# Products of a differential head issued one per tile, its outputs kept two tiles later

## The reference

```
s1 = q1 @ k1.T * scale;  s2 = q2 @ k2.T * scale          # inner width 64
p  = softmax(s1) - lam * softmax(s2)
d_out = p @ v                                            # [512, 128] a head
d_out = rms_norm(d_out, subln_g) * (1 - lambda_init)
mix = concat([mla_out, d_out]) @ w_out
```

## Time and profile before

| | us |
|---|---|
| median of three runs | 1977.25 |
| lowest and highest of them | 1976.67, 1977.47 |
| the profiled execution | 1974.83 |
| its span, first to last instruction | 1973.0 |
| busy: PE, DVE, ACT, POOL | 1890.3, 775.5, 610.6, 627.3 |
| mean granted clock of PE | 0.996 |

### The profile page before, as it was taken

How to read it: one execution, slowest core, us unless ns; L and a number is a source line. 1 busy time by engine, 2 the same in 40 slices (tenths; PEclk the granted TensorE clock), 3 DMA queues, 4 the chain that set the end, 5 groups by cost and what they waited for, 6 DMA issues and landing times.

```text
span 1973.0 us, 22515 instructions
## 1 busy us (share of the span) xinstructions
PE 1890.3 (96%) x8888; PEld 1242.0 (63%) x8888; DVE 775.5 (39%) x1568; ACT 610.6 (31%) x1111; POOL 627.3 (32%) x374
## 2 busy tenths in 40 slices
PE   9999989999898989989999999999999999999998
PEld 7554547533333333368887868655677678888786
DVE  6663476422222222352899225477341120000002
ACT  2112762201101101062224334477344242222213
POOL 0000532011101101064433324566443335455532
PEclk9999999999999999999999999999999999999999
DMA  9651033899999999952224321110232023223221
GB/s 388 258 180 45 27 112 149 312 386 426 428 427 428 428 429 427 379 213 86 86 88 126 108 85 54 65 33 23 87 138 86 22 78 125 86 85 99 115 85 64
DMA packets 90055, 358.33 MB, mean 182 GB/s; under 512 B 6971, under 2 KB 35899, under 8 KB 75500
## 3 DMA queue, kind: packets, MB, share of 16 engines
q1 hardware_dynamic: 87104, 351.75, 46.1%
q0 software_dynamic: 2304, 4.20, 0.6%
q10 hardware_dynamic: 556, 1.13, 0.2%
HBM read 355.42 MB, written 5.83 MB: 183 GB/s over the span
## 4 chain that ended last, share of the span: by engine, by line
PE 77%; DMA 13%; DVE 4%; ACT 2%; POOL 1%; issue 1%; SPq 0%; POOLq 0%; ACTq 0%; DVEq 0%
PE bank L774 15%; PE bank L775 14%; PE bank L776 14%; PE bank L749 10%; DMA slots<-in_w_expert_gate 9%; PE bank L1210 7%; DMA slots<-in_w_expert_up 3%; PE bank L1412 2%; PE bank L1423 2%; PE bank L1443 2%; PE bank L917 1%; PE bank L1181 1%; PE bank L1235 1%; PE bank L1182 1%; DMA slots<-in_w_ada 1%
## 5 line engine op out<-in xcount | busy, mean ns | idle before, releaser
L2909 POOL TENSOR_TENSOR low_r<-slots,high_r 128x2048 fp32r<-128x2048 f32 x82 | 378.6, 4618 | 514.5 <-ACT high_r L1662 514.5
L775 PE MATMUL bank<-xl_r,high_r 128*128 128x512 f32 (+1 forms) x832 | 320.3, 385 | 0.0
L774 PE MATMUL bank<-area_r,high_r 128*128 128x512 f32 x800 | 312.6, 391 | 0.0
L776 PE MATMUL bank<-area_r,low_r 128*128 128x512 f32 x800 | 311.3, 389 | 0.0
L1662 ACT ACTIVATE high_r<-slots 128x2048 fp32r<-128x2048 f32 x82 | 156.9, 1914 | 405.4 <-PE bank L776 404.1
L1210 PE MATMUL bank<-slots,area 128*64 128x512 f32 x992 | 226.8, 601 | 22.8 <-DMA slots<-in_w_expert_gate 16.5
L775 PEld LDWEIGHTS bank<-xl_r,high_r 128*128 128x128 f32 x832 | 156.3, 188 | 31.4 <-issue 0.5
L1210 PEld LDWEIGHTS bank<-slots,area 128*64 128x64 f32 x992 | 67.5, 137 | 165.7 <-issue 126.1
L774 PEld LDWEIGHTS bank<-area_r,high_r 128*128 128x128 f32 x800 | 150.2, 188 | 31.7 <-issue 0.6
L776 PEld LDWEIGHTS bank<-area_r,low_r 128*128 128x128 f32 x800 | 150.2, 188 | 31.3
L2710 DVE SCALAR_TENSOR_TENSOR bank<-area,cols,bank 128x512 f32<-128x512 f32 x232 | 153.4, 741 | 0.0
(11 more groups left out here) (434 smaller groups left out, 2848.5 us busy)
## 6 DMA issues: line engine op xcount, KB each, us to landing
slots<-in_w_expert_down SPq DMA_DIRECT2D x32, 2048.0 KB, 16.2
slots<-in_w_expert_up SPq DMA_DIRECT2D x32, 2048.0 KB, 16.1
slots<-in_w_expert_gate SPq DMA_DIRECT2D x30, 2048.0 KB, 15.0
slots<-in_w_in SPq DMA_DIRECT2D x14, 2048.0 KB, 8.2
slots<-in_w_ada SPq DMA_DIRECT2D x11, 2048.0 KB, 12.2
slots<-in_ffn_in_w SPq DMA_DIRECT2D x22, 1024.0 KB, 7.1
slots<-in_ffn_out_w SPq DMA_DIRECT2D x5, 2048.0 KB, 7.8
slots<-in_w_out SPq DMA_DIRECT2D x4, 2048.0 KB, 8.0
```

Source lines behind the costliest of these rows:

```text
L774: nc.tensor.matmul(out, xh, yh, start=start and n == 0, stop=False)
L775: nc.tensor.matmul(out, xh, yl, start=False, stop=False)
L776: last = nc.tensor.matmul(out, xl, yh, start=False, stop=stop and n == len(pairs) - 1)
L2909: nc.gpsimd.tensor_tensor(low_half(m), raw_half(m), high_half(m), ALU.subtract).then_inc(s["w_low"], 1)
```

## The change

On PE, the products of heads 3 to 5 no longer stand as a block of four behind the transposes of tiles 17, 21 and 25. They go one per tile, at tiles 17 to 20 (head 3), 21 to 24 (head 4) and 25 to 28 (head 5), between `scores(t + 3)` and the wait for the probabilities of t. Head 6 has only three tiles left, 29 to 31, and does two, one and one. Heads 0 to 2 and head 7 stay as they were. On ACT the outputs of heads 3, 4 and 5 are kept at tile 21, 25 and 29 instead of 19, 23 and 27, and those of head 6 still at 31. The split of head 3 moves to tile 21, and its low part on POOL from tile 21 to tile 23.

```diff
-            def outputs(h):
-
-                pe.wait_ge(s["pt_ready"], TT * (h + 1))
-                if h >= 2:
-                    pe.wait_ge(s["pv_emptied"], h - 1)
+            def outputs(h, first=0, end=TT):
+
+                if first == 0:
+                    pe.wait_ge(s["pt_ready"], TT * (h + 1))
+                    if h >= 2:
+                        pe.wait_ge(s["pv_emptied"], h - 1)
                 V, c0 = (VM, h * P) if h < 4 else (DV, (h - 4) * P)
-                accumulate(banks[h % 2][:, :], [(V[:, j, c0:c0 + P], PT[h % 2][:, j, :]) for j in range(TT)]
-                           ).then_inc(s["pv_full"], 1)
+                for j in range(first, end):
+                    last = nc.tensor.matmul(banks[h % 2][:, :], V[:, j, c0:c0 + P], PT[h % 2][:, j, :], start=j == 0,
+                                            stop=j == TT - 1)
+                if end == TT:
+                    last.then_inc(s["pv_full"], 1)
...
+                h, part = (t - 1) // TT - 1, (t - 1) % TT
+                if 3 <= h < 6:
+                    outputs(h, part, part + 1)
+                elif h == 6:
+                    outputs(h, part + (part > 0), part + 2)
                 if t < 16:
                     pe.wait_ge(s["probs_mla"], t + 1)
...
-                if t >= 5 and t % TT == 1:
-                    outputs(t // TT - 1)
+                if 0 <= h < 3 and part == 0:
+                    outputs(h)
...
-                if t >= 7 and t % TT == 3:
+                if t in (7, 11, 15):
                     keep_outputs(t // TT - 1)
-                    if t // TT - 1 < 4:
-                        split_head(t // TT - 1)
+                    split_head(t // TT - 1)
+                if t in (21, 25, 29):
+                    keep_outputs(t // TT - 2)
+                if t == 21:
+                    split_head(3)
+                if t == 31:
+                    keep_outputs(6)
...
-                if t >= 9 and t % TT == 1 and t // TT <= 5:
+                if t in (9, 13, 17):
                     low_head(t // TT - 2)
+                if t == 23:
+                    low_head(3)
```

## The result

| | us |
|---|---|
| before, median of 19 runs | 1976.24 (1974.02 to 1979.13) |
| changed, median of 19 runs | 1978.45 (1976.33 to 1983.38) |
| ratio, changed to before | 1.0014, interval 1.0008 to 1.0021 |
| profiled execution, changed | 1979.44, span 1977.6, mean clock 0.994 |

The kernel is slower by 0.14%, some 2.8 us (the medians differ by 2.2), where 0.9 us of gain was forecast. The spans differ by 4.6 us, but not all of it lies in the stage: the scores of tile 20 start at 240.09 here and at 237.34 before, so 2.75 us were lost ahead of the stage, in code that both kernels share. I therefore read the stage from those scores to the first product of head 7, as the prediction did. After it is 287.34 - 240.09 = 47.25. The stage alone is **1.74 us longer**.

A forecast was written before the change was run, and what follows sets the result against it. Waits between engines, with none full, were taken to bound the stage; keeping outputs only moves the stall. Head 7's products start at 281.99 instead of 282.85, so 1977.25 - 0.86 gives 1976.4 us, range 1974.0 to 1978.8.

The forecast's parts named there:

- Bounds and program order: First attention, tiles 16 to 31: no engine full, waits decide; ACT's keeping ahead of tile 22's exponentials holds up PE's scores.
- The first rival: Tiles 18 to 29: keeping holds back no exponential, 2.50 us a tile, about 6 us kept, 1971.3 us; chance 0.08.
- PE now stands still once a head for the keeping: Before the scores of tiles 24 and 28: the stall only moves, PE waiting 1.5 to 1.6 us for exponentials.
- the piece: One product of a head on PE, behind a tile's scores: taken as 0.91 us, bounds 0.86 and 1.06.
- its end: From the end of a head's last piece on PE to ACT's keeping: 0.11 us.
- the chain of a head: Pieces and transposes to the last piece, keeping, exponentials, scores: 12.05 us a head against 12.03 before, bounds 11.6 and 12.8.
- the schedule: Hand schedule from tile 20's scores at 237.34: scores of 24 at 249.09, head 7's products at 281.99 against 282.85.
- The change of tiling mode: Switching PE between 128 and 64 rows costs 0.05 to 0.09 us; without cost a tile is 2.36, gain 2.3 us.
- The end: Before head 7: ACT keeps head 6 (0.97 us), then two tiles of PT; head 7's products start at 281.99.
- The third: Rival, tiles with pieces: pieces 1.06, transposes 0.59, tile 2.71, period 12.8 us; 1978.8 us, no gain; chance 0.22.
- The second: Rival, tiles 21 to 31: late exponentials split score pairs, up to 0.66 us each; 5 us slower, 1982.3; chance 0.06.
- the shift reaches the end whole: From head 7 on all is PE's chain and transfers wait for PE, so the 0.86 us gain reaches the end.

The follow-up runs named there:

- e7: Changed kernel with head 3's copy and split later, heads 4 and 5 squared and copied in separate later tiles, head 6 kept last; ratio to before 0.9968.
- e1: The changed kernel run again without any edit; ratio to before 1.0014, stage 47.25 us.
- e6: Changed kernel with head 6's keeping moved behind the last two keeps of PT; ratio to before 1.0001, stage 46.28 us.
- e8: The kernel before, unedited, profiled a second time; stage 45.51 us, no ratio given.
- e4: Kernel before with only the late keeping of heads 3 to 5, products still in a block; ratio to before 0.9999, stage 45.82 us.
- e5: Kernel before with 6 unread products of ones in its 1.53 us wait ahead of tile 29's transposes; ratio 1.0001, stage 45.51 us.
- e2: Changed kernel with unread products of ones filling four PE waits; ratio to before 0.9989, stage 45.66 us.
- e9: Repeat of the changed kernel with four PE waits filled by unread products; ratio to before 0.9991, stage 45.66 us.
- e11: Changed kernel with only the two waits before the scores of tiles 24 and 28 filled; ratio to before 0.9981, stage 45.66 us.
- e3: Changed kernel with heads 3 to 5 kept one ACT tile later, at 22, 26 and 30; ratio to before 0.9984, stage 41.50 us.
- e10: Changed kernel with later, spread keeping, and each product of heads 3 to 6 behind its tile's transposes; ratio to before 0.9977, stage 38.94 us.
- e12: Repeat of the changed kernel with later, spread keeping and head 6 kept last; ratio to before 0.9958, stage 38.87 us.

## Why the prediction was wrong

**Bounds and program order: right.** No engine was full, and the keeping ahead of the exponentials moved the stall as described. PE waits 1.58 and 1.40 us (1.5 to 1.6 forecast), ACT 1.52 (about 1.5). The first rival, PE running through if the keeping held back no exponential, had the transposes of tile 29 start 32.2 us behind the scores of tile 20 (237.34 to 269.5). e7 makes that order of ACT, and there it is 32.5 us (237.08 to 269.58), against 38.1 before. So the condition named for that rival was the right one, and so was the reason given against it here, ACT's program order.

**The step that failed: "PE now stands still once a head for the keeping".** The stall was counted by its length alone. What it does to PE's clock wasn't asked, with the clock in the row beside it. In all three profiles of this order (the changed kernel, e1, e6) the clock fell once, at the first or the second of the two stalls; in the eleven profiles without a stall of that length ahead of a score pair it never fell in the stage (before, e8, e4 and e5, the fillings e2, e9 and e11, and e3, e7, e10 and e12). One fall costs 1.6 us, and filling the stalls gives it back. Of the miss in the stage, from -0.86 to +1.74, this is 1.59.

**The terms that were mis-sized: the piece, and its end.** 0.91 was taken for a piece, 0.96 measured (241.33 to 242.29), inside the bounds of 0.86 and 1.06. From the start of what follows a last piece to ACT it is 0.20 instead of 0.11 (249.95 to 250.15): a piece ends 1.12 us after its start, so its end lies 0.16 behind the next start, where the block's lay 0.07 behind. Four pieces and one such end make 0.3 us a head. In e2, without a fall, the chain of a head measures 12.34 us (250.72 to 263.06) where the sum has 12.05 and before has 12.03. The same 0.3 is lost on the way to the first stall (12.03 from the scores of 20 to those of 24, where the schedule has 11.75) and from the second to the transposes of 29 (14.07 for 13.76), and 0.13 by the last product of head 6. Together this is the other 1.01 us of the miss. So the sign was lost already without the clock: 45.66 against 45.51. The transposes at 0.53, the pair at 1.06, the square and the copy at 0.97 and the 0.66 by which a second half comes late were right.

**The change of tiling mode.** With no cost for it a tile was to be 2.36 us and the gain 2.3 us. The measured tile is 2.55: 0.10 us more for the piece between 64-row scores and transposes (0.96 for 0.86) and 0.09 for the transposes ahead of 64-row scores (0.53 for 0.44). The Trainium skill (TensorEngine Tiling, Key Properties) says that such a change drains TensorE. The trace agrees in that there is a cost at each; that a drain is what makes it, it can't show.

**The end** was right in its shape: head 6's keeping ahead of the last two PT keeps costs what it was put at; e6 takes 0.97 us of it back.

**Rivals.** The third (dear pieces, 1978.8) came nearest in time, for a reason only partly its own: pieces cost 0.96, not 1.06, and transposes 0.53, not 0.59. The second didn't occur; in every steady tile a score pair took 1.13. A clock that falls wasn't among the rivals and should have been. That 1978.45 lies inside the range of 1974.0 to 1978.8 is luck: its upper end is the third rival's, reckoned from a median of three runs that is 1.0 us above that of nineteen, and 1.6 us of the loss came from something that no term of the range stands for.

**What lies behind the stage.** That the shift reaches the end whole could not be seen in single profiles: the rest, from head 7's first product to the end of the span, is 1690.2 us before and 1690.3 after, but 1691.6 in e8 and 1691.3 in e1. The medians' 2.2 us and the ratio's 2.8 stand 0.5 to 1 us above the stage's 1.74, within the interval.

**Left open.** The filled versions have a rest of 1688.3, 1688.3 and 1688.5 us in their three profiles, some 2 us less than the others' 1689.0 to 1692.2, and that would put them 0.1 to 0.2% below before. In the profiles the rest goes with the clock, which falls at a few places where PE has gaps (around 368, 850 and 1236 us; in e2 PE is busy 1.5 us of the four from 1232, at a mean clock of 0.77) in some executions and not in others. The four shortest rests are those of the four profiles that lack a fall around 368 (e2) or around 1236 (e5, e9 and e11); the other ten have both, and 1689.9 us or more. But that is fourteen single executions, and over all of them the mean clock of the filled versions is that of before (0.9951 over 34, 0.9952 over 92). So it isn't shown that the filling at 250 us changes those falls, and what the 2 us are was not found. Nor was it found how long or how empty a wait must be for the clock to fall.

## What to carry to other kernels

When products are dealt out over the tiles to fill holes, the consumer of their sum must be moved behind the last piece in its own engine's order, so that it never waits for it: one tile in ACT's list decided between 0.14% slower and 0.16% faster, and spreading the copies made it 0.3 to 0.4%. Look at which instruction stands directly behind a waiting one, and who needs it next. And a stall of PE has two prices, its length and what it does to the clock: read the granted clock behind every stall that a change leaves or makes, and give the fall a rival of its own.

## What the runs showed of the hardware

A wait of PE of 1.4 to 1.6 us cost the clock at one place and not at another. In the changed order it fell once in each of three profiles, at one of two like stalls (1.58 and 1.40 us), with 1.6 us lost. In the same stage waits of 1.41 and 1.72 us at its end, of 1.53 us in the kernel before and of 1.86 us in e4 had no fall behind them, in eight profiles. Behind the two bad stalls comes a score pair whose second half waits again (1.72 us instead of 1.06), behind the others whole products or transposes. Whether that is what tells them apart wasn't tried; the length of the wait alone doesn't, and in each of the three profiles the clock held at the other of the two.

Score pairs of 64 rows, side by side, keep their 1.06 us to the next start whether transposes or whole products stand around them (242.82 to 243.88 after; 243.09 to 244.15 in e10). A whole product costs 0.86 us inside a block and 0.96 alone, on either side of the transposes (241.33 to 242.29 after; 242.13 to 243.09 in e10). Four transposes cost 0.53 us ahead of score pairs, 0.49 between scores and a product (241.64 to 242.13 in e10) and 0.44 between products.
